# Eight loads of condition weights issued by ScalarE instead of the sync engine

## The reference

```
mod = silu(c) @ w_cond + b_cond          # c: 2 rows; w_cond: 1024 x 6144
shift_m, scale_m, gate_m, shift_f, scale_f, gate_f = split(mod, 6)
h   = LN(x) * (1 + scale_m) + shift_m
mix = token_mixer(h)                     # projections w_in, gated linear and stick-breaking attention
x   = LN1(alpha * x + gate_m * mix)
h   = LN(x) * (1 + scale_f) + shift_f
x   = LN2(alpha * x + gate_f * hier_moe(h))   # 32 experts, two for each token
```

## Time and profile before

| | |
|---|---|
| device time, 3 runs | 1044.6, 1045.94, 1047.01 us |
| span of the profiled execution, first to last instruction | 1044.5 us |
| device time of the profiled execution itself | not given apart from its span |
| TensorE busy | 941.7 us, 90% of the span |
| VectorE, ScalarE, GpSimd busy | 435.7, 278.0, 319.4 us |
| DMA moved | 294.08 MB, 282 GB/s over the span |
| loads of `cond_slot` | 9 of 2048 KB, median 11.9 us from issue to landing |
| gate stage | about 257 to 405 us of the span |

### The profile page before, as it was taken

The page is one execution under the profiler, slowest core; times in us unless marked ns, Lnnn a source line. Parts: engine busy times, 40 slices in busy tenths (PEclk is TensorE's granted clock), DMA queues, the critical chain, the costliest instruction groups (busy, mean ns, idle before and its releaser), DMA issues.

```text
span 1044.5 us, 14674 instructions
## 1 busy us (share of the span) xinstructions
PE 941.7 (90%) x5901; PEld 626.2 (60%) x5913; DVE 435.7 (42%) x884; ACT 278.0 (27%) x466; POOL 319.4 (31%) x268
## 2 busy tenths in 40 slices
PE   4999998999997999999999999999988888988975
PEld 3789998896997988898643444444433333433321
DVE  4201188816541336868953333333323223223215
ACT  1463433351675567433340000000000000000100
POOL 7655477760432433570001111111111111111010
PEclk9999999999999999999999999999999999999997
DMA  9971544438577582387597999999999999999833
GB/s 328 327 143 45 103 105 115 82 85 248 154 160 243 145 269 88 126 297 282 235 387 305 422 424 427 425 425 425 426 425 426 426 427 425 428 423 424 373 116 122
DMA packets 61030, 294.08 MB, mean 282 GB/s; under 512 B 7493, under 2 KB 9133, under 8 KB 48114
## 3 DMA queue, kind: packets, MB, share of 16 engines
q1 hardware_dynamic: 49584, 272.68, 70.5%
q0 software_dynamic: 6480, 11.40, 3.3%
q10 hardware_dynamic: 4914, 9.28, 2.4%
HBM read 289.97 MB, written 14.68 MB: 292 GB/s over the span
## 4 chain that ended last, share of the span: by engine, by line
PE 53%; DMA 29%; DVE 8%; ACT 4%; issue 3%; POOL 2%; SPq 1%; POOLq 0%; ACTq 0%; DVEq 0%
DMA ring<-in_w_exp_up 18%; PE bank L1457 15%; PE bank L1097 6%; PE bank L1480 6%; PE bank L1099 6%; PE bank L1098 6%; DMA ring<-in_w_in 5%; DMA cond_slot<-in_w_cond 4%; PE bank L1048 1%; PE bank L1447 1%; PE bank L1469 1%; DVE hf L2021 1%; DVE out_lo L1821 1%; POOL w_lo L566 1%; ACT hf L958 1%
## 5 line engine op out<-in xcount | busy, mean ns | idle before, releaser
L1457 PE MATMUL bank<-ring,hf 128*64 128x512 f32 x992 | 222.3, 600 | 22.3 <-DMA ring<-in_w_exp_up 22.1
L566 POOL TENSOR_TENSOR w_lo<-ring,w_hi 128x1024 fp32r<-128x1024 f32 x76 | 183.9, 2431 | 169.9 <-ACT w_hi L771 169.9
L1097 PE MATMUL bank<-h_hi,w_hi 128*128 128x320 f32 x576 | 184.1, 320 | 7.8 <-POOL w_lo L566 5.4
L1099 PE MATMUL bank<-h_hi,w_lo 128*128 128x320 f32 x576 | 179.1, 311 | 0.0
L1457 PEld LDWEIGHTS bank<-ring,hf 128*64 128x64 f32 x992 | 76.6, 139 | 165.3 <-issue 148.8
L958 ACT ACTIVATE hf<-bank 64x512 f32<-64x512 f32 x31 | 18.2, 588 | 431.3 <-PE bank L1457 431.3
L1480 PE MATMUL bank<-ring,he 128*64 128x512 f32 x512 | 128.4, 647 | 0.7 <-DVE he L2025 0.5
L1098 PE MATMUL bank<-h_lo,w_hi 128*128 128x320 f32 x384 | 119.8, 312 | 0.0
L1097 PEld LDWEIGHTS bank<-h_hi,w_hi 128*128 128x128 f32 x576 | 109.3, 190 | 14.3 <-issue 8.5
L1099 PEld LDWEIGHTS bank<-h_hi,w_lo 128*128 128x128 f32 x576 | 109.3, 190 | 0.0
L616 POOL DMA_INDIRECT xrow<-expert_inputs,sidx x31 | 31.7, 1024 | 250.7 <-DVE sidx L1999 229.3
(11 more groups left out here) (405 smaller groups left out, 1307.5 us busy)
## 6 DMA issues: line engine op xcount, KB each, us to landing
ring<-in_w_exp_down SPq DMA_DIRECT2D x32, 2048.0 KB, 31.5
ring<-in_w_exp_gate SPq DMA_DIRECT2D x31, 2048.0 KB, 29.7
ring<-in_w_exp_up SPq DMA_DIRECT2D x31, 2048.0 KB, 34.4
ring<-in_w_in SPq DMA_DIRECT2D x15, 2048.0 KB, 15.9
cond_slot<-in_w_cond SPq DMA_DIRECT2D x9, 2048.0 KB, 11.9
ring<-in_w_cond SPq DMA_DIRECT2D x3, 2048.0 KB, 17.3
ring<-in_w_branch_b SPq DMA_DIRECT2D x2, 2048.0 KB, 8.0
ring<-in_w_branch_a SPq DMA_DIRECT2D x2, 2048.0 KB, 11.3
```

Of the source, the lines that this page charges most:

```text
L566: pool.tensor_tensor(w_lo_of[slot][:, :, c], raw[:, :, c], w_hi[:, :, c].bitcast(F32), ALU.subtract)\
L1097: mm(b, hi[:, k, c], x_hi[:, k, :], start=(k == 0), stop=False)
L1099: last = mm(b, lo[:, k, c], x_hi[:, k, :], start=False, stop=(k == KT - 1))
L1457: last = mm(bank[1][64 * q:64 * q + 64, :], xg[:, k % 4, k // 4, :], ring[s + q][:, k * FF:k * FF + FF], start=(k == 0), stop=(k == KT - 1 ...
```

## The change

The loads of chunks 4 to 11 leave SP's list. ScalarE issues chunk 4 behind its waits for the stage before, ahead of the attention steps, and each following one right behind its copy of turned rows (`ct`) of the chunk before. What is loaded, where to, and the semaphore of its landing are the same. SP keeps its order for all other chunks.

```diff
+        def weight_rows(name, c0):
+            return SRC[name].rearrange("(k p) n -> p k n", p=P)[:, :, c0:c0 + CB]
...
                 before = [n for n in range(i) if DENSE[n][2] == slot]
+                if slot == COND_SLOT and before:
+                    continue
                 if before:
                     sp.wait_ge(*consumed(before[-1]))
-                if slot == COND_SLOT and len(before) == 1:
-                    sp.wait_ge(S["go_ps"], 6)
-                    sp.wait_ge(S["st_ready"], 4)
...
+            def cond_load(c):
+                act.dma_start(cond_slot[:, :].rearrange("p (k n) -> p k n", k=KT), weight_rows("cond", c * CB))\
+                    .then_inc(S["cond_in"], 16)
...
                 ins.then_inc(S["taken_act"], 1)
                 g[0] += 1
+                if name == "ct" and 4 <= i < 11:
+                    cond_load(i + 1)
...
             act.wait_ge(S["go_ps"], 6)
+            act.wait_ge(S["st_ready"], 4)
+            cond_load(4)
             act.wait_ge(S["gla_stored"], 16 * 6)
```

More of the change, by code:

```diff
@@ L434, in _ @@
                     sp.wait_ge(S["on_t"], KT)
-                src = SRC[name].rearrange("(k p) n -> p k n", p=P)[:, :, c0:c0 + CB]
+                src = weight_rows(name, c0)
                 dst = cond_slot if slot == COND_SLOT else ring[slot]
```

## The result

The changed kernel is slower: 1056.22 us, median of 9 runs, beside 1046.05 us, median of 9 runs of the kernel before. The ratio is 1.0089, 95% interval 1.0058 to 1.0120, or +6.1 to +12.5 us; 1052.4 was forecast. One of the nine runs was slow (1120.54 us, at a granted clock of 0.825) and is left out of the ratio. The median lies 3.8 us above the forecast, inside the range of all (1045.5 to 1057.0) and just outside the forecast's own (1049 to 1056). The profiled execution has a span of 1056.9 us, 12.4 more than that of before.

The account below looks back on a forecast made before the run. TensorE's chain was taken as the bound, with late condition chunks in the gate stage delaying the end. Terms -0.3 + 2.5 + 2.8 + 1.5 = +6.5 us gave 1052.4 us; own range 1049 to 1056, range of all 1045.5 to 1057.0.

Parts of the forecast that it names:

- Chunk 4: Gate stage: issued at 258.3, landing 8.2 us later at 266.5, making its product 0.8 us late (0.4 to 1.2).
- Chunk 6: Gate stage: issued behind a weight copy that waits for a ring load, costing +0.6 us (0 to 1.5).
- that load was ahead of chunk 6 in the queue and gains nothing: Premise that the ring load of 278.83 lands no sooner once the chunk is issued later, at 292.4.
- Chunk 7: Gate stage: landing at 322.6 instead of 322.8, so TensorE idles 3.6 us instead of 5.40.
- S: How late TensorE is against before; forecast at -0.3 us behind chunk 7's wait.
- The standing: ScalarE's queue gets no packets behind a ring load at first, as a store stood 7.4 us in the earlier trace.
- 6.1 us "of its own": Time chunk 7 was taken to need from 316.0 on, 322.8 less 316.7, giving a landing at 322.6.
- Rival A: Both DMA queues share from the issue on: chunk 7 lands at 318.7, sum +0.1, 1046.0 us; chance 0.14.
- Chunk 8: Gate stage: issued 1.4 us after a ring load instead of ahead, landing at 344 to 345, cost +2.5 us.
- The low end: Lower bound for chunk 8: both loads at the free rate, landing at 343.4, cost +1.4 us.
- The clock: TensorE's lower clock after idling: one loss kept and one added, +1.5 us (-1.6 to +3.1).
- Chunk 10: Gate stage: issued at 373.7 behind a delayed weight copy, landing 381.9, net +2.8 us (up to +6.5).
- rival B: Ring loads land sooner without a chunk behind them, one needing under 13.5 us: sum -4.2, 1041.7 us; chance 0.07.

Follow-up runs that it names:

- second profile: The changed kernel profiled again with no edit: 1061.58 us, a span of 1059.8 us.
- exchanged order: The kernel before with chunk 7 put ahead of the ring load in SP's list: ratio 0.9942; profiled again, 1044.66 us.

## Why the prediction held, term by term

The direction, the stage and the gate stage's sum were right: +6.5 forecast, +6.3 at the branch end in the first profile. That the sum is so near is luck, for errors cancel in it: 1.3 us too little up to chunk 7 and 1.8 too little at chunk 8 stand against 3.3 too much at chunk 10. In the second profile it was +9.8.

*Chunk 4:* +0.8 forecast, +1.5 measured. The issue was on time (258.73, less the 0.7 of start); the load took 9.1 us, not the 8.2 of the quiet one. *Chunk 5:* 0, as forecast. *Chunk 6:* +0.6 forecast, 0 in the first profile, +3.6 in the second. The step that failed there is "that load was ahead of chunk 6 in the queue and gains nothing": with the chunk no longer 5.4 us behind it the load took 11.0 us in the second profile in place of 12.4, and that lets GpSimd meet VectorE.

*Chunk 7:* a saving was forecast that swallows the lateness so far (S = -0.3); measured 1.0, so the wait swallowed 0.4 of 1.4. The standing was right, and the store of the earlier trace rows foretold it: no packet for 8 us. The sharing behind it was not: q10 started when the ring load had 0.17 MB left, and the chunk landed at 324.5 (323.8 less the start), 5.9 us behind the ring load, instead of 322.6. So it came as if it stood strictly behind, just past the upper bound of 323.6. The step that failed is the 6.1 us "of its own" from 316.0 on: in the trace before they run from the ring load's landing and move only the last 1.54 MB of that chunk. The rule of the Trainium skill ("DMA: Bandwidth & Descriptors", "Queues, rings and completion order"), taking turns a packet at a time, agrees with chunk 8 from 336 us on (49% and 54%), but not with its first 4 us (0.14 MB of q10 beside 0.54 of q1 from 332 to 336) and not with chunk 7 from its issue on. Rival A, which rested on it, failed at this place.

*Chunk 8:* +2.5 forecast, +4.3 up to its product. This is the mis-sized term: the forecast had 344 to 345, and the chunk landed at 347.8 (347.1 less the start). The low end took the same 6.1 us, the tail of a chunk, for each of two whole loads; together the two needed 15.7 us, where it had reckoned 13.2 (1 us and twice 6.1). *The clock:* one loss more was forecast, put at chunk 10 in the working; it came behind chunk 8, 1.6 us, after 4.1 us of idling.

*Chunk 10:* +2.8 was forecast; measured -0.5. Two premises failed: that the ring load "comes no earlier" (14.4 us, not 16.6; in five of the seven profiles with the chunk issued 5.4 us behind it 16.5 to 17.4, and 15.2 in the other two, both of the exchanged order; in the seven with the chunk 9.6 us behind it or later 14.4 to 15.7), and that the issue follows the copy (it went out 0.96 us ahead of it). This is the half of rival B that was true, though the load did not fall under the 13.5 us that B asked for.

*To the end.* That the lateness passes on whole is borne out by eight profiles with the clock kept in the router stage: branch end against end of span, -3.0 and -3.4, +12.0 and +12.1, +5.8 and +6.3, +1.1 and +1.3, +0.3 and +0.3 agree within 0.5 us; +4.9 and +3.5, +2.9 and +4.8, +7.4 and +5.9 only within 2. What the forecast lacked is the 5.6 us between the branch products and the experts in the changed kernel's profiles (5.1 in the second), nearly all at the lower clock.

## What to carry to other kernels

When a load moves to another issuer, ask first what it was ahead of: here one chunk of eight lost a head start of 3.7 us on a ring load and made nearly the whole loss of the gate stage in the first profile, while queue and issuer cost nothing by themselves. Look at the same place for the order that gains: exchanging two entries of a list, so that the load that is waited for goes ahead of the one with slack, was worth 6 us. And ask what an earlier landing sets free: a ring load 1.5 us quicker brought two engines together and cost 3.5 us. Last, a sum that comes out right proves no term; the terms are checked one by one against the trace.

## What the runs showed of the hardware

- A DMA issued by ScalarE goes out while the activations listed before it still run: 0.96 us ahead of the copy that stands before it in the list.
- VectorE's step on 128x512 took 2.72 instead of 0.69 us when GpSimd's 128x1024 subtraction had started 0.2 us before it; so it went in all 53 such meetings of fourteen profiles (2.7 to 2.9 us), and in none of the 171 steps without one. A ring load 1.5 us quicker was enough to bring the two together.
- A ring load landed sooner when no condition chunk was issued 5.4 us behind it: 10.7 to 11.0 us in six of seven profiles, instead of 12.2 to 13.2 in all seven with one.
- 1 KB issued by ScalarE behind a ring load on SP's queue took 12.0 us to land; the quickest of the eight such loads took 4.0. A chunk of 2 MB in that place had no packet for 8 us.
